# Bounding the accumulating scatter of expert rows at the last token

## The reference

```
scores = sigmoid(x1 @ w_router);  each token picks 6 of 64 experts, weights normalised * 2.5
for each expert e, for each token t that picked it:
    h = silu(x1[t] @ we_gate[e]) * (x1[t] @ we_up[e])         # 1024 -> 256
    routed[t] += weight[t, e] * (h @ we_down[e])               # 256 -> 1024
out = LayerNorm(alpha * x1 + routed + shared_expert(x1))
```

## Time and profile before

| | |
|---|---|
| median of 3 runs | 1694.11 us |
| profiled execution | 1695.34 us |
| its span, first to last instruction | 1693.5 us |
| PE busy | 91% of the span |
| DVE, ACT, POOL busy | 48%, 24%, 26% |
| moved by DMA | 317.69 MB, 188 GB/s over the span |
| mixture of experts, first scatter to load of the sum | 944.5 to 1660.1 us |

### The profile page before, as it was taken

One profiled execution on the slowest core, in us unless ns is written; L12 is line 12 of the kernel. 1 busy time (PEld: TensorE's weight loads), 2 busy tenths in 40 slices (PEclk: granted clock), 3 DMA queues, 4 the chain that ended last, 5 costly groups with the idle time before them and its releaser, 6 DMA issues. The chain is left out here.

```text
span 1693.5 us, 18624 instructions
## 1 busy us (share of the span) xinstructions
PE 1540.6 (91%) x5878; PEld 867.6 (51%) x5878; DVE 804.7 (48%) x1586; ACT 403.6 (24%) x702; POOL 433.0 (26%) x444
## 2 busy tenths in 40 slices
PE   7997999999999975899998999999999999999990
PEld 4544777777777762355543444444444444444440
DVE  1362766676676645258854333333333333333335
ACT  1302553555465431122200100111001100111015
POOL 0000000000000000004344455555555555555530
PEclk9995999999999986899999999999999999999995
DMA  9006000000000008100146899999999999999955
GB/s 247 13 25 74 7 11 19 8 16 13 17 7 7 14 11 299 63 26 26 53 189 252 306 369 368 365 363 365 370 362 361 367 363 361 360 363 372 331 146 211
DMA packets 106205, 317.69 MB, mean 188 GB/s; under 512 B 39382, under 2 KB 56430, under 8 KB 81170
## 3 DMA queue, kind: packets, MB, share of 16 engines
q1 hardware_dynamic: 81570, 257.27, 40.7%
q0 software_dynamic: 23408, 59.45, 14.5%
q10 hardware_dynamic: 1152, 0.00, 0.0%
HBM read 271.73 MB, written 51.72 MB: 191 GB/s over the span
## 5 line engine op out<-in xcount | busy, mean ns | idle before, releaser
L1555 PE MATMUL moe_p_gu<-mixers_ring,moe_xgT 128*128 128x512 f32 x784 | 344.6, 592 | 0.0
L1686 DVE STREAM_TRANSPOSE moe_xgT<-moe_xg 128x1024 f32<-128x1024 f32 x65 | 132.0, 2031 | 423.2 <-DMA moe_xg<-x_d,moe_idx 423.2
L1501 POOL DMA_INDIRECT moe_xg<-x_d,moe_idx x260 | 263.6, 1014 | 116.1 <-issue 60.1
L1128 POOL DMA_INDIRECT slot_d<-all_entry,all_dest_i x48 | 48.0, 1000 | 824.5 <-DVE all_dest_i L1340 812.3
L1575 PE MATMUL moe_p_y<-mixers_ring,moe_hT 128*128 128x512 f32 x520 | 233.9, 592 | 0.9 <-DVE moe_hT L1697 0.9
L1555 PEld LDWEIGHTS moe_p_gu<-mixers_ring,moe_xgT 128*128 128x128 f32 x784 | 145.7, 191 | 164.5 <-issue 164.5
L1512 POOL DMA_INDIRECT sum_d<-moe_y,moe_idx x65 | 105.4, 1622 | 246.3 <-DMA sum_d<-moe_y,moe_idx 208.9
L1623 ACT ACTIVATE moe_sig<-moe_p_gu 128x256 f32<-128x256 f32 x65 | 25.0, 384 | 584.6 <-PE moe_p_gu L1555 584.6
L1575 PEld LDWEIGHTS moe_p_y<-mixers_ring,moe_hT 128*128 128x128 f32 x520 | 98.7, 190 | 125.0 <-issue 123.9
L677 PE MATMUL att_p_o<-att_v,att_prT 128*128 128x64 f32 x1024 | 129.0, 280 | 20.7 <-ACT att_prT L764 18.5
L677 PEld LDWEIGHTS att_p_o<-att_v,att_prT 128*128 128x128 f32 x1024 | 122.5, 196 | 32.8 <-ACT att_prT L764 30.4
(11 more groups left out here) (307 smaller groups left out, 1859.9 us busy)
## 6 DMA issues: line engine op xcount, KB each, us to landing
mixers_ring<-in_we_down_dram SPq DMA_DIRECT2D x65, 1024.0 KB, 8.2
mixers_ring<-in_we_gate_dram SPq DMA_DIRECT2D x49, 1024.0 KB, 9.9
mixers_ring<-in_we_up_dram SPq DMA_DIRECT2D x49, 1024.0 KB, 14.7
mixers_o<-in_we_gate_dram SPq DMA_DIRECT2D x16, 1024.0 KB, 9.6
mixers_o<-in_we_up_dram SPq DMA_DIRECT2D x16, 1024.0 KB, 14.5
moe_xg<-x_d,moe_idx POOLq DMA_INDIRECT x260, 6.8
all_x_sb<-in_x_dram SPq DMA_DIRECT2D x8, 512.0 KB, 12.0
mixers_ring<-in_w_o_dram SPq DMA_DIRECT2D x1, 4096.0 KB, 22.3
```

Of the source, the lines that this page charges most:

```text
L1501: nc.gpsimd.indirect_dma_start(xg[:, u, g, :], None, x1_quarters, bass.IndirectOffsetOnAxis(ap=idx[:, c, g:g + 1], axis=0), bounds_check=N ...
L1555: last = nc.tensor.matmul(p_gu[:, u, :], xgT[:, u, kk, :], k.moe_gu[v][:, :, kk * F:(kk + 1) * F], start=(kk == 0), stop=(kk == KD - 1))
L1686: nc.vector.transpose(xgT[:, u].rearrange("p k (g i) -> p g k i", g=NQ), xg[:, u].rearrange("p g (j k) -> p g k j", k=KD)).then_inc(x_turn ...
```

## The change

Two edits. The sum loses its 128 spare rows. The accumulating scatter gets a bound: an index above 1023 is out of range, and its row is left out without an error. The indices of blank slots (1024 to 1151) stay as they are, so every blank slot's row is now out of range. Waits, order, buffers and all other instructions stay.

```diff
@@ persistent
-    k.sum_d = nc.dram_tensor("sum_d", (SEQ + P, D), f32).ap()
+    k.sum_d = nc.dram_tensor("sum_d", (SEQ, D), f32).ap()
@@ moe_experts, gpsimd, scatter
                 nc.gpsimd.indirect_dma_start(k.sum_d[:, :], bass.IndirectOffsetOnAxis(ap=idx[:, c, NQ:NQ + 1], axis=0),
-                                             y[:, u, :], None, compute_op=ALU.add).then_inc(y_out, 16)
+                                             y[:, u, :], None, bounds_check=SEQ - 1, oob_is_err=False,
+                                             compute_op=ALU.add).then_inc(y_out, 16)
```

## The result

The changed kernel is slower. Its median over four runs is 1706.16 us (1700.44 to 1706.36), beside 1692.52 us over four runs of the kernel before; the ratio is 1.0074, 95% interval 1.0052 to 1.0096. Run again beside the experiments it gave 1706.06 us and 1.0073 (1.0049 to 1.0096). The forecast was 1692 us, range 1672 to 1702. Every run here is in the same state, but for one run of 9114.86 us of the kernel that relieves the other half, which is left out.

A forecast was written before the change was run, and what follows sets the result against it. The prediction took the chain of accumulating scatter landings, set by the slowest DMA engine, to bound the kernel. Terms of -4 us (less traffic), +2 us (bound) and 0 (smaller tensor, tail) gave -2 us: 1692 us from 1694.11, range 1672 to 1702.

The forecast's parts named there:

- The chain of scatters is the bound: Expert stage: accumulating scatters land one after another, 56 steps of 11.21 us, 35% of the span.
- The bytes left out: POOL's queue: 2176 blank scattered rows (26%) go, so it moves 50.5 MB instead of 59.45.
- The runs of four slots on an engine: Scatter: an engine's packet holds four neighbouring slots, so 32 blanks touch at most 8 engines; at least 8 keep eight rows.
- A: The forecast: full engines set the scatter's landing, 10.3 to 10.5 us; 1692 us, own range 1687 to 1698, chance 0.68.
- B: Rival: the scatter's landing follows the amount moved; 34 to 38 us gained, 1656 to 1660 us; chance 0.14.
- The tail: Late scatters: the lone one keeps eight rows on full engines, the last one is hidden; 0 us.
- None of the three terms changes on a full engine: A full engine's step: weight packets 7.8 us, eight rows 2.4 us, gathers and closing packets 1.3 us, all unchanged.
- term (a): Shared memory traffic: 3.2% fewer bytes per step help full engines by 0.07 us, -4 us over 56 steps.
- term (b): POOL between landing and next start: register move and bounded issue add 0.07 us a step, 0 to 4 us, +2 taken.
- C: Rival: in the scatter a dropped row is not free or the bound slows descriptors; up to 17 us slower, 1711; chance 0.13.
- its weaker form: Rival on the scatter's landing: it gains only the 3.2% of bytes, 0.36 us a step, 20 us, giving 1674 us.

The follow-up runs named there:

- the kernel that relieves the other half: The changed kernel with each block's ranks turned by 64 slots (rank r to slot (r + 64) mod 128), so blanks are slots 32 to 63: 1710.31 us, ratio 1.0104.
- the bound alone: The kernel before plus a scatter bound at the last spare row, spare rows kept, so all 128 rows travel: 1694.74 us, ratio 0.9995.
- run 50: Not a run number: the text reads "repeated run 50% and 42%", shares for the changed kernel run again beside the experiments, 1706.06 us, ratio 1.0073 to the kernel before.
- one full engine: The changed kernel with slots 32-63 and 96-127 dropped except 32-35, so one engine has eight rows, fifteen four: 1714.06 us, ratio 1.0123 to the kernel before.

## Why the prediction was wrong

**What held.** The chain of scatters is the bound, and its step follows the slowest engine. The bytes left out came out as counted. The runs of four slots on an engine, read off the gathers' small packets, are borne out by what follows from them: the same rows dropped in a different place move the time from 1.007 to 0.989, and one run of four more leaves one engine behind. The median landing stayed at 10.4 us and the chain did not go over to PE, as A said and B did not. The tail gave nothing, as said. The Trainium skill's rule that a DMA costs a fixed part and its bytes ("DMA: Bandwidth & Descriptors", "Anatomy of one DMA — SWDGE (gpsimd) path") would have been 17 us of gain; the runs go against it here, as 64 rows in one place are slower than 128 spread over all.

**What failed.** The step "None of the three terms changes on a full engine", and with it the small term (a). I took the full engines to be no worse off when their neighbours are relieved, and let them even profit from 3.2% less traffic, -4 us. It was the wrong sign. These are the first and the 56th scatter, both on the chain, in the changed kernel and then in its repeated run:

```profile
941.30 10.94 DMA sum_d<-moe_y,moe_idx
1564.05 10.17 DMA sum_d<-moe_y,moe_idx
```

```profile
943.13 10.84 DMA sum_d<-moe_y,moe_idx
1568.31 10.15 DMA sum_d<-moe_y,moe_idx
```

A step went from 11.21 to 11.32 us in the first (1564.05 - 941.30 over 55) and to 11.37 in the second, above the 11.1 to 11.25 that the prediction named as its sign of being right. That is +6 to +9 us, and the last nine blocks add 2 to 2.5 us. With the bound alone a step is 11.20 us, so the dropped rows cost 0.12 to 0.17 us in each step where term (a) had a gain of 0.07.

The sum of an engine's packets did not see this, since the landing also depends on the order in which the two queues are served. The packet records of the traces show some of it. They do not name the engine, but they can be chained, since on an engine one packet starts as the one before it ends. I took 49 scatters of each kernel, the fifth to the 53rd. Before the change, of the rows that start 7 to 8 us after their scatter, 68% follow another row and 30% follow a weight packet. In the changed kernel 41% and 52% do, in its repeated run 50% and 42%. So more rows now wait for a weight packet.

But the last engine took turns already: in 37 of the 49 scatters before the change the last eight rows can be chained with a weight packet ahead of each, as at the full engine above. Its eight rows took about 5.0 us before and take it now. What moved is when they begin. In the scatters that can be chained so (37, 24, 27, 12 and 14 of 49, in the order of the figures that follow), the first of the eight rows starts 5.09 us after the scatter before the change and 4.99 with the bound alone, but 5.11 and 5.15 in the two runs of the changed kernel and 5.37 with one full engine. With the gap of 0.80 us before the change and 0.87 in the others, counted from the landing ahead, that is 5.89 and 5.86 against 5.98, 6.02 and 6.24 us, in the same order as the steps of 11.21, 11.20, 11.32, 11.37 and 11.50 us. In these scatters the engine that ends last reaches its rows later; it does not write them more slowly.

**The term (b)** was sized well (0.07 us a turn) and has no price here: 0.9995 with the bound alone. Half of it was taken, +2 us.

**The rivals.** C named slower, 1711 us, but by a dropped row or a bound that costs by itself. The bound alone costs nothing, and dropped rows gain when they are spread. B would have had the right direction had the slots been dealt out evenly, but half of its size: that kernel exists now and gives 1675 us, 18 us less than the kernel before, where B had 34 to 38 and its weaker form 20. Its engines still hold six rows and its landing is 9.8 us, so PE does not lead yet.

**What stays open.** That relief of only some engines slows the kernel is shown (1.0074, 1.0104, 1.0123 for scatters, 1.0066 for gathers), and that the loss goes away with lighter weight loads. Why the last engine reaches its rows later when other engines are relieved isn't. The later landings of the weight loads, 12.3 and 19.5 us, suggest that the relieved engines end their part early and the full ones fall behind with more weight packets queued. A cost for each change between queues on a filled engine, or the restart of the relieved engines' loads, would both fit, and no run here separates them.

## What to carry to other kernels

A scatter has landed when its last engine is done: one engine with eight rows beside fifteen with four made the slowest kernel here. Before leaving rows out, ask which engine each row lies on, and drop them evenly; the size and the mean share of the engines say nothing about that. Where two queues share filled engines, relieving some of them can delay the others, so a saving in the wrong place may cost time. And a small delay ahead of a long wait can be absorbed by it, as the 0.07 us was here: look at the landing behind a gap before pricing the gap.

## What the hardware showed that was not expected

- Four rows of 4 KB on one of 16 engines moved the kernel from 0.980 to 1.012, 58 us, 0.9 us in each of some 64 blocks.
- Accumulating rows of 4 KB start 0.31 us apart on their engine when nothing else runs, and 0.63 us apart when they take turns with 8 KB weight packets.
- Dropped rows stay as tiny packets: the changed kernel has as many packets as before on POOL's queue (23408 in both). By which rows are dropped, the kernel gained up to 2.0% or lost up to 1.2%.
- A register move and its issue, 0.07 us in each of 65 turns on the chain, cost nothing, and taking it away again gained nothing.
